# The up-projection's matmuls in six orders of 64-byte blocks, and operands at other distances from the weights

## The chip, the cores and the metric

The kernel runs on one core of a Trainium2 chip. The metric is the device time of one execution in microseconds (us). A core has a matrix engine (TensorE, "PE" in the profile, with "PEld" for its weight loads), a vector engine (VectorE, "DVE"), a scalar engine (ScalarE, "ACT"), GpSimd ("POOL") and a queue engine (SyncE, "SP") that issues the transfers. They work from an on-chip memory of 128 partitions; TensorE writes to the accumulation banks ("bank" and "sm" in the program), from which VectorE and ScalarE read.

## The reference

One layer of a decoder trunk on 256 tokens of width 2048, all float32. The sandwich of each sub-layer is norm, sub-layer, norm, residual:

```python
    h = rms_norm(x, ln_mix_pre[l])
    y = hybrid_mixer(h, positions, w_in[l], ...)          # four mixers, gates, w_branch, w_out
    x = x + rms_norm(y, ln_mix_post[l])
    h = rms_norm(x, ln_mem_q[l])
    y = memory_cross_attention(h, rms_norm(mem, ln_mem_kv[l]), mem_wq[l], mem_wkv[l], mem_wo[l])
    x = x + rms_norm(y, ln_mem_post[l])
    h = rms_norm(x, ln_ffn_pre[l])
    y = conv_ffn(h, ffn_w_up[l], ffn_conv_w[l], ffn_conv_b[l], ffn_w_down[l])
    x = x + rms_norm(y, ln_ffn_post[l])

def conv_ffn(h, w_up, w_conv, b_conv, w_down):
    u = causal_dwconv(h @ w_up, w_conv) + b_conv
    a, b = jnp.split(u, 2, axis=-1)
    return (jax.nn.gelu(a, approximate=True) * b) @ w_down
```

The up-projection `h @ w_up` is 2048 by 11264, in 88 chunks of 128 output channels.

## The kernel before

The kernel streams some 390 MB of weights once, in chunks of 2048 x 128 numbers (1 MB), numbered by `m` from the input projection to the down-projection. SyncE loads a chunk in two halves `h` of 512 KB into `raw`. ScalarE (L1274) rounds a half to the format `fp32r` ("high"), VectorE (L1977, in `low`) subtracts that from the original ("low"). Both parts go to one of four slots, `wsplit[(2 * m + h) % 4]`, each with 8 high blocks of 128 columns and 8 low ones. The activations are split likewise into 256 high and 256 low columns per block of 128 channels, side by side: `H` for the mixing stage, `X1` for W_out, the query projection and the up-projection, `X2` for the memory keys and the cross-attention's output projection (X2 also holds the memory that the values read).

There are two kinds of chunk. Where the weights are the stationary operand, a half is 8 wide matmuls (high weights times high and low activations, 512 columns, L543 in the mixing stage and L1008 behind it) and 8 narrow ones (low weights times high activations, 256 columns, L546 and L1017), added up in one accumulation bank. A chunk's halves run as high 0, low 0, low 1, high 1, so narrow and wide ones alternate in groups of sixteen. Where the output is wanted by tokens (retention values, gates, branches, memory values, down-projection), the activations are the stationary operand and the weights move: 512 columns each, L427 to L430, L1104 to L1106, L1221 to L1223.

The sequence on each engine is written out by hand, and semaphores tie them: `hi_done` and `lo_done` when a slot's part is ready, `half_used` when TensorE has read a half, `prod_out` when VectorE has taken a result out of its bank. The up-projection's chunks 0 and 1 are written apart (L1175 and L1178), 2 and 3 call `chunk`, and 84 more run in `loop(M_UP + 4, 21, X1)`, four chunks to a round. `chunk` calls `products`, that `high_products` and `low_products`.

Places are given in words of 4 bytes from `region_at`, a multiple of 1024 bytes. The slots start at 4096, 6144, 8192 and 10240, `H` at 12288, `X1` at 22288, `X2` at 35136. Blocks follow at 128 words in a slot, and at 512 words in an activation. Modulo 256 bytes all slots, H and X2 therefore lie at 0 and X1 at 64: the distance of the moving operand from the weights, modulo 256 bytes, is 64 with X1 and 0 with H and X2.

## Time and profile before

| | us |
|---|---|
| median of 3 runs (2188.47 to 2188.89) | 2188.55 |
| the profiled execution | 2189.49 |
| its span, first to last instruction | 2187.7 |
| TensorE busy in the span | 2161.2 |
| VectorE busy | 1439.2 |
| ScalarE busy | 1065.3 |
| wide matmuls of L1008, 2336 of them, busy | 563.9 |
| narrow matmuls of L1017, 2336 of them, busy | 296.4 |

The busy time of a group counts overlapping records once; the recorded duration of one matmul (392 ns for a wide one) reaches past the start of the next, since matmuls are pipelined. The distance from start to start tells what a matmul costs the engine: for sixteen in a row, the start of the group behind them minus their own.

### The profile page before, as it was taken

The page shows a single profiled execution, that of the slowest core. Times are in us where ns is not written, and L with a number is a line of the kernel's source. Part 1 is how long each engine was busy: PE and PEld are TensorE (multiplying, and loading weights), DVE is VectorE, ACT ScalarE, POOL GpSimd, SP SyncE. Part 2 cuts the span into 40 slices and gives each one's busy share as a digit, 9 for nine tenths or more (in the row PEclk, how much of TensorE's full clock was granted, in tenths as well). Part 3 has the DMA queues.
Part 4 walks back from the last instruction along what each step waited for, and adds up shares of the span by engine and source line. Part 5 has one row for each costly group of instructions (what it writes and reads, how often), then busy time and mean ns, then how long its engine had stood idle before and what let it go on. Part 6 is the DMA issues. An engine that isn't in the chain of part 4 may idle for free.

```text
span 2187.7 us, 33212 instructions
## 1 busy us (share of the span) xinstructions
PE 2161.2 (99%) x12606; PEld 1840.3 (84%) x12606; DVE 1439.2 (66%) x1651; ACT 1065.3 (49%) x1438; POOL 244.9 (11%) x220
## 2 busy tenths in 40 slices
PE   7999999999999999999999999989999999999998
PEld 6888888788888888888888888878888888888887
DVE  7986658676554546467765544578778777876444
ACT  6452245446444444445444444456656555644443
POOL 1132000000000101025110001312111111100000
PEclk9999999999999999999999999999999999999999
DMA  7543344445666665675556643636556555656664
GB/s 266 173 149 113 119 149 153 136 153 184 194 191 192 191 194 190 195 265 184 185 186 193 192 151 114 198 115 209 188 184 196 191 190 184 193 191 212 193 192 153
DMA packets 107071, 393.83 MB, mean 180 GB/s; under 512 B 11888, under 2 KB 12144, under 8 KB 106576
## 3 DMA queue, kind: packets, MB, share of 16 engines
q1 hardware_dynamic: 106672, 391.10, 55.5%
q8 instruction: 78, 1.28, 0.2%
q10 hardware_dynamic: 288, 1.18, 0.2%
q14 instruction: 33, 0.27, 0.0%
HBM read 390.14 MB, written 2.10 MB: 179 GB/s over the span
## 4 chain that ended last, share of the span: by engine, by line
PE 94%; DVE 3%; ACT 1%; DMA 1%; issue 1%; SPq 0%; DVEq 0%; ACTq 0%
PE bank L1008 24%; PE bank L1017 12%; PE bank L543 7%; PE sm L429 5%; PE sm L430 5%; PE sm L427 5%; PE bank L546 4%; PE bank L1221 3%; PE bank L1223 3%; PE bank L1222 3%; PE bank L427 2%; PE bank L429 2%; PE bank L430 2%; PE sm L595 2%; PE bank L1106 1%; PE bank L1105 1%
## 5 line engine op out<-in xcount | busy, mean ns | idle before, releaser
L1977 DVE TENSOR_TENSOR part<-part,part 128x1024 fp32r<-128x1024 f32 x724 | 933.5, 1292 | 527.6 <-ACT part L1274 516.7
L1274 ACT ACTIVATE part<-part 128x1024 fp32r<-128x1024 f32 x724 | 763.9, 1058 | 578.0 <-PE sm L430 177.6
L1008 PE MATMUL bank<-part,part 128*128 128x512 f32 x2336 | 563.9, 392 | 0.1
L1008 PEld LDWEIGHTS bank<-part,part 128*128 128x128 f32 x2336 | 427.9, 188 | 84.4 <-issue 0.5
L1017 PEld LDWEIGHTS bank<-part,part 128*128 128x128 f32 x2336 | 293.5, 188 | 12.4
L1017 PE MATMUL bank<-part,part 128*128 128x256 f32 x2336 | 296.4, 279 | 0.0
L543 PE MATMUL bank<-part,part 128*128 128x512 f32 x832 | 207.3, 396 | 0.9 <-DVE part L2032 0.8
L427 PE MATMUL sm<-part,part 128*128 128x512 f32 x512 | 199.2, 389 | 0.0
L429 PE MATMUL sm<-part,part 128*128 128x512 f32 x512 | 199.2, 389 | 0.0
L430 PE MATMUL sm<-part,part 128*128 128x512 f32 x512 | 199.2, 389 | 0.0
L543 PEld LDWEIGHTS bank<-part,part 128*128 128x128 f32 x832 | 151.5, 188 | 33.2 <-issue 2.1
L1596 ACT ACTIVATE part<-bank 128x256 f32<-128x256 f32 x152 | 58.1, 382 | 165.9 <-PE bank L1008 147.6
L1221 PE MATMUL bank<-part,part 128*128 128x512 f32 x352 | 137.2, 390 | 0.6 <-DVE part L2738 0.6
L1223 PE MATMUL bank<-part,part 128*128 128x512 f32 x352 | 137.0, 389 | 0.0
L1222 PE MATMUL bank<-part,part 128*128 128x512 f32 x352 | 136.9, 389 | 0.0
L546 PE MATMUL bank<-part,part 128*128 128x256 f32 x832 | 114.1, 286 | 2.5 <-DVE part L1977 2.4
L546 PEld LDWEIGHTS bank<-part,part 128*128 128x128 f32 x832 | 108.1, 191 | 9.8 <-issue 2.7
L427 PEld LDWEIGHTS sm<-part,part 128*128 128x128 f32 x512 | 96.1, 188 | 20.1
L429 PEld LDWEIGHTS sm<-part,part 128*128 128x128 f32 x512 | 96.1, 188 | 19.9
L430 PEld LDWEIGHTS sm<-part,part 128*128 128x128 f32 x512 | 96.1, 188 | 19.9
L2554 DVE TENSOR_TENSOR part<-bank,part 128x256 f32<-128x256 f32 x152 | 64.3, 423 | 71.9 <-ACT part L1596 71.6
L427 PE MATMUL bank<-part,part 128*128 128x512 f32 x224 | 90.3, 403 | 0.0
(382 smaller groups left out, 2204.4 us busy)
## 6 DMA issues: line engine op xcount, KB each, us to landing
part<-in_w_up SPq DMA_DIRECT2D x176, 512.0 KB, 4.5
part<-in_w_gate SPq DMA_DIRECT2D x128, 512.0 KB, 4.5
part<-in_w_dn SPq DMA_DIRECT2D x88, 512.0 KB, 4.5
part<-in_w_br SPq DMA_DIRECT2D x40, 512.0 KB, 4.5
part<-in_w_out SPq DMA_DIRECT2D x32, 512.0 KB, 4.7
part<-in_w_mk SPq DMA_DIRECT2D x32, 512.0 KB, 4.6
part<-in_w_mv SPq DMA_DIRECT2D x32, 512.0 KB, 4.2
part<-in_w_q SPq DMA_DIRECT2D x32, 512.0 KB, 4.3
```

What stands on the lines that cost most here:

```text
L427: pe.matmul(dst, xh, w[:, 0, j, :], start=first and h == 0 and j == 0, stop=False, skip_group_check=True)
L429: pe.matmul(dst, xh, w[:, 1, j, :], start=False, stop=False, skip_group_check=True)
L430: mm = pe.matmul(dst, xl, w[:, 0, j, :], start=False, stop=last and h == 1 and j == 1, skip_group_check=True)
L543: mm = pe.matmul(b, w[:, 0, k, :], H[:, 8 * h + k, :], start=h == 0 and k == 0, stop=h == 1 and k == 7, skip_group_check=True)
L546: mm = pe.matmul(b[:, T:2 * T], w[:, 1, k, :], H[:, 8 * h + k, 0:T], start=False, stop=False, skip_group_check=True)
L1008: mm = pe.matmul(dst, w[:, 0, k, :], x[:, k0 + k, :], start=start and k == 0, stop=stop and k == n - 1, skip_group_check=True)
L1017: mm = pe.matmul(dst[:, T:2 * T], w[:, 1, k, :], x[:, k0 + k, 0:T], start=False, stop=stop and k == n - 1, skip_group_check=True)
L1221: pe.matmul(bank[:, s, :], x, w[:, 0, j, :], start=k0 + j == 0, stop=False, skip_group_check=True)
L1222: pe.matmul(bank[:, s, :], x, w[:, 1, j, :], start=False, stop=False, skip_group_check=True)
L1223: mm = pe.matmul(bank[:, s, :], g[:, k + j, T + s * P:T + (s + 1) * P], w[:, 0, j, :], start=False, stop=k0 + j == FT - 1, skip_group_chec ...
L1274: act.activation(wsplit[(2 * m + h) % 4][:, 0, 0:n, :], raw[:, m % 2, h, 0:n, :], cp) .then_inc(sem("hi_done"), 1)
L1977: tt(w[:, 1, 0:n, :], raw[:, m % 2, h, 0:n, :], w[:, 0, 0:n, :].bitcast(f32), SUB).then_inc(sem("lo_done"), 1)
```

## The change

Three things are changed.

The orders: `chunk` and what it calls take a number `order`. `reordered` lays it over the moving operand and, in the same way, over the output, so that each column's sum lands where it did. Order 0 is the old one; 1 runs through all columns backwards; 2 swaps neighbouring blocks of 16 columns (64 bytes); 3 reverses each four blocks; 4 takes every fourth block, four times; 5 takes the even blocks, then the odd ones. The up-projection's loop runs 14 rounds of six chunks, one in each order, instead of 21 rounds of four.

The distances: a slot is now a place of 2112 words, and `parts` puts its contents at its start, or 48 words (192 bytes) behind it. At the start they lie in chunks in which the weights move (`by_tokens`, the compression chunks too) and in the second half of each chunk of the up-projection and of the first two of the down-projection. In all others they lie 192 bytes behind, and the distance of the moving operand is 64 bytes modulo 256. `X1` moves by 16 words, `X2` and others by 64 or 16, `raw` to 1024 bytes ahead of the region, and the region itself to a multiple of 256 bytes. So the first half of an up-projection chunk has the distance 64 and the second half 0; W_out and query chunks have 64 as before; the mixing chunks with H and the X2 chunks have 64 instead of 0.

Nothing is changed in what is loaded, split, waited for or written out.

```diff
+def by_tokens(m):
+    return m < NMIX and MIX[m][0] in ("rv", "gate", "br", "cmp") or M_MV <= m < M_WQ or m >= M_DOWN + 2
...
-        region_at = -(-nc.sbuf_base // 1024) * 1024
+        region_at = -(-nc.sbuf_base // 256) * 256 + 1024
...
-        raw = part(0, 2, 2, 8, P)
-        wsplit = [partr(8192, 2, 8, P), partr(10240, 2, 8, P), partr(4096, 2, 8, P), partr(6144, 2, 8, P)]
+        raw = part(-256, 2, 2, 8, P)
+        slots = [partr(a, 2112) for a in (8064, 10176, 3840, 5952)]
+
+        def parts(m, h):
+
+            s = slots[(2 * m + h) % 4]
+            aligned = by_tokens(m) or M_UP <= m < M_DOWN + 2 and h == 1
+            return (s[:, 0:2048] if aligned else s[:, 48:2096]).rearrange("p (l k c) -> p l k c", l=2, c=P)
...
-        X1 = partr(22288, KT, 2 * T)
+        X1 = partr(22272, KT, 2 * T)
...
-        X2 = partr(35136, 20, 2 * T)
+        X2 = partr(35072, 20, 2 * T)
...
+            def reordered(v, order):
+
+                if order == 1:
+                    return v[:, ::-1]
+                if order == 2:
+                    return v.rearrange("p (a b c) -> p a b c", b=2, c=16)[:, :, ::-1, :]
+                if order == 3:
+                    return v.rearrange("p (a b c) -> p a b c", b=4, c=16)[:, :, ::-1, :]
+                if order == 4:
+                    return v.rearrange("p (a b c) -> p b a c", b=4, c=16)
+                if order == 5:
+                    return v.rearrange("p (a b c) -> p b a c", b=2, c=16)
+                return v
...
-                w = wsplit[(2 * m + h) % 4]
+                w = parts(m, h)
                 for k in range(n):
-                    mm = pe.matmul(dst, w[:, 0, k, :], x[:, k0 + k, :], start=start and k == 0,
+                    mm = pe.matmul(reordered(dst, order), w[:, 0, k, :], reordered(x[:, k0 + k, :], order),
...
+                    mm = pe.matmul(reordered(dst[:, T:2 * T], order), w[:, 1, k, :],
+                                   reordered(x[:, k0 + k, 0:T], order), start=False,
...
-            loop(M_WO + 4, 3, X2)
+            loop(M_WO + 4, 3, X2, (0, 0, 0, 0))
...
-            loop(M_UP + 4, 21, X1)
+            loop(M_UP + 4, 14, X1, (0, 1, 2, 3, 4, 5))
```

TensorE's loop over the up-projection, a round's third and fourth chunk before (`part_68` is X1, `part_52` and `part_53` are the two slots of an odd chunk, `part_50` and `part_51` those of an even one):

```order
L1008 MATMUL bank<-part_68,part_50 128x512 x8
L1017 MATMUL bank<-part_68,part_50 128x256 x8
L1014 REGISTER_ALU
L1017 MATMUL bank<-part_68,part_51 128x256 x8
L1008 MATMUL bank<-part_68,part_51 128x512 x8
L1034 REGISTER_ALU
L1005 REGISTER_ALU
L1008 MATMUL bank<-part_68,part_52 128x512 x8
L1017 MATMUL bank<-part_68,part_52 128x256 x8
```

The same place in the changed kernel, a round's third chunk (order 2) and the start of its fourth (order 3):

```order
L1034 MATMUL bank<-part_68,part_50 128x16x2x16 x8
L1043 MATMUL bank<-part_68,part_50 128x8x2x16 x8
L1040 REGISTER_ALU
L1043 MATMUL bank<-part_68,part_51 128x8x2x16 x8
L1034 MATMUL bank<-part_68,part_51 128x16x2x16 x8
L1061 REGISTER_ALU
L1031 REGISTER_ALU
L1034 MATMUL bank<-part_68,part_52 128x8x4x16 x8
L1043 MATMUL bank<-part_68,part_52 128x4x4x16 x8
```

No instruction moves; only the operands' shapes become those of blocks (the reversed order reads like order 0 in such a row). The end of the round, changed kernel, orders 4 and 5:

```order
L1034 MATMUL bank<-part_68,part_50 128x4x8x16 x8
L1043 MATMUL bank<-part_68,part_50 128x4x4x16 x8
L1040 REGISTER_ALU
L1043 MATMUL bank<-part_68,part_51 128x4x4x16 x8
L1034 MATMUL bank<-part_68,part_51 128x4x8x16 x8
L1061 REGISTER_ALU
L1031 REGISTER_ALU
L1034 MATMUL bank<-part_68,part_52 128x2x16x16 x8
L1043 MATMUL bank<-part_68,part_52 128x2x8x16 x8
L1040 REGISTER_ALU
L1043 MATMUL bank<-part_68,part_53 128x2x8x16 x8
L1034 MATMUL bank<-part_68,part_53 128x2x16x16 x8
```

These two chunks follow four others in a round, where before the round ended after its fourth chunk.

## Rows read from the trace of the kernel before

**Rows 1.** the page: busy us (share of the span), granted clock by slice, chain by engine and line

```profile
PE 2161.2 (99%) x12606; PEld 1840.3 (84%) x12606; DVE 1439.2 (66%) x1651; ACT 1065.3 (49%) x1438; POOL 244.9 (11%) x220
PEclk9999999999999999999999999999999999999999
PE 94%; DVE 3%; ACT 1%; DMA 1%; issue 1%; SPq 0%; DVEq 0%; ACTq 0%
PE bank L1008 24%; PE bank L1017 12%; PE bank L543 7%; PE sm L429 5%; PE sm L430 5%; PE sm L427 5%; PE bank L546 4%; PE bank L1221 3%; PE bank L1223 3%; PE bank L1222 3%; PE bank L427 2%; PE bank L429 2%; PE bank L430 2%; PE sm L595 2%; PE bank L1106 1%; PE bank L1105 1%
```

**Rows 2.** busy us (count) of each engine in the up loop

```profile
core 0: us, PE busy (x) PEld busy (x) DVE busy (x) ACT busy (x) POOL busy (x), PEclk, DMA share, GB/s
1480.00:1938.00 458.00, 458.00 (x2658) 402.98 (x2657) 363.39 (x505) 274.15 (x418) 67.18 (x84) 1.00 0.60 192
```

**Rows 3.** waits in the same stretch: who for whom, us in total, times, longest

```profile
engine line waited for: us in total, times, longest us
...
DVE part L1977 <- ACT part L1274: 42.8, 72, 2.5
ACT part L1274 <- PE bank L1017: 37.0, 60, 0.9
```

**Rows 4.** TensorE in order of time, up loop (moving operand X1)

```profile
start us, us, engine line op out<-in xcount [idle before <-releaser]
1496.27 3.82 PE L1008 MATMUL bank<-part,part 128*128 128x512 f32 x16
1499.93 2.04 PE L1017 MATMUL bank<-part,part 128*128 128x256 f32 x16
1501.82 3.84 PE L1008 MATMUL bank<-part,part 128*128 128x512 f32 x16
1505.49 1.98 PE L1017 MATMUL bank<-part,part 128*128 128x256 f32 x16
1507.31 3.82 PE L1008 MATMUL bank<-part,part 128*128 128x512 f32 x16
1510.96 2.05 PE L1017 MATMUL bank<-part,part 128*128 128x256 f32 x16
1512.85 3.84 PE L1008 MATMUL bank<-part,part 128*128 128x512 f32 x16
1516.53 1.98 PE L1017 MATMUL bank<-part,part 128*128 128x256 f32 x16
1518.34 3.82 PE L1008 MATMUL bank<-part,part 128*128 128x512 f32 x16
1522.00 2.05 PE L1017 MATMUL bank<-part,part 128*128 128x256 f32 x16
```

**Rows 5.** the same, memory-key stage (moving operand X2)

```profile
1071.58 3.82 PE L1008 MATMUL bank<-part,part 128*128 128x512 f32 x16
1075.24 2.08 PE L1017 MATMUL bank<-part,part 128*128 128x256 f32 x16
1077.15 3.82 PE L1008 MATMUL bank<-part,part 128*128 128x512 f32 x16
1080.80 2.08 PE L1017 MATMUL bank<-part,part 128*128 128x256 f32 x16
1082.72 3.82 PE L1008 MATMUL bank<-part,part 128*128 128x512 f32 x16
```

**Rows 6.** the same, mixing stage (moving operand H)

```profile
484.89 3.82 PE L543 MATMUL bank<-part,part 128*128 128x512 f32 x16
488.55 2.08 PE L546 MATMUL bank<-part,part 128*128 128x256 f32 x16
490.46 3.82 PE L543 MATMUL bank<-part,part 128*128 128x512 f32 x16
494.11 2.08 PE L546 MATMUL bank<-part,part 128*128 128x256 f32 x16
```

**Rows 7.** the same, matmuls in which the weights are the moving operand

```profile
850.25 0.39 PE L427 MATMUL bank<-part,part 128*128 128x512 f32 x1
850.48 0.39 PE L429 MATMUL bank<-part,part 128*128 128x512 f32 x1
850.70 0.39 PE L430 MATMUL bank<-part,part 128*128 128x512 f32 x1
850.93 0.39 PE L427 MATMUL bank<-part,part 128*128 128x512 f32 x1
```

**Rows 8.** chain of 1338 to 1345 us, plain float32 matmuls: start, us, what

```profile
1340.62 3.47 PE sm L1127 x16
```

**Rows 9.** all weight loads of L1017: duration ns min/median/max, first and last start

```profile
L1017 PEld LDWEIGHTS bank<-part,part x2336: 187/188/192, 960.9 to 1937.4; 128*128 128x128 f32 x195
```

**Rows 10.** the wide matmuls of the mixing stage, whole span: busy us, mean ns | idle

```profile
L543 PE MATMUL bank<-part,part 128*128 128x512 f32 x832 | 207.3, 396 | 0.9 <-DVE part L2032 0.8
L555 PE MATMUL bank<-part,part 128*128 128x512 f32 x32 | 10.1, 466 | 8.8 <-ACT part L1274 8.3 <-DVE part L2090 0.5
```

**Rows 11.** chain of 1354 to 1361 us, groups of four after an interruption

```profile
1355.41 0.92 PE bank L1047 x4
1356.33 0.47 PE bank L1049 x4
1356.81 0.93 PE bank L1047 x4
1357.73 0.47 PE bank L1049 x4
1358.20 0.93 PE bank L1047 x4
```

More of the change, by code:

```diff
@@ L560, in first_low @@
                 for k in range(8 * h, 8 * h + 8):
-                    mm = pe.matmul(bank[:, n, T:2 * T], wsplit[2 * n + h][:, 1, k % 8, :], H[:, k, 0:T], start=False,
+                    mm = pe.matmul(bank[:, n, T:2 * T], parts(n, h)[:, 1, k % 8, :], H[:, k, 0:T], start=False,
                                    stop=h == 1 and k == 15, skip_group_check=True)
@@ L1034, in chunk @@
                 pe.wait_ge(prod_out, at(1, m - R_OFF - 1))
[L1035 removed]
+                products(m, at, x, 0, 8, x, 8, 8, bank[:, m % 2, :], split=split, order=order)
             def half(m, h, x, start=False, stop=False):
@@ L1067, in two_chunks, with loop @@
                 quarter(m + 1, 3, x).then_inc(half_used, 2)
-            def loop(base, count, x):
+            def loop(base, count, x, orders):
+                n = len(orders)
                 with pe.Fori(0, count) as i:
-                    for j in range(4):
-                        chunk(base + j, lambda k, v: i * (4 * k) + v, x)
+                    for j in range(n):
+                        chunk(base + j, lambda k, v: i * (n * k) + v, x, order=orders[j])
             def y_norm(value):
```

66 lines of the change are left out of this document (32 added, 34 removed).

## The prediction

> **What bounds the kernel now.** I began with the page's busy shares and chain [rows 1]: TensorE is busy for 2161.2 of 2187.7 us at full granted clock (2.4 GHz), and its matmuls are 94% of the chain. A matmul's recorded duration overlaps its successor's, so I work from starts. In the loop of the up-projection (1480 to 1938 us) TensorE is busy in all 458.00 us with 2658 matmuls, 32 to a chunk: 458/83.06 = 5.51 us a chunk [rows 2]. VectorE is busy 363 us there, ScalarE 274, the DMA engines 60%. Their own waits (VectorE L1977 for ScalarE 42.8 us, ScalarE L1274 for TensorE 37.0) show slack, and no wait of TensorE is in that list [rows 3]. So each nanosecond of a matmul's step, start to next start, is on the path, 16 times 512 columns and 16 times 256 per chunk.
>
> Three sets of steps matter. They differ in where the moving operand lies against the weights, counted in bytes modulo 256:
> - up loop, X1, +64 bytes. Starts 1505.49, 1507.31, 1510.96, 1512.85, 1516.53 [rows 4]: sixteen narrow steps 1.82, sixteen wide 3.65, then 1.89 and 3.68 (five chunks stand there, and they alternate so). Two chunks 11.04 us, **5.52 a chunk**.
> - memory-key stage, X2, 0 bytes: 3.66 and 1.91 each time, from 1071.58 to 1082.72 two chunks 11.14, **5.57 a chunk** [rows 5].
> - mixing stage, H, also 0 bytes: 1.91 and 3.65, together 5.56 [rows 6]. X2 is 256 bytes off H modulo 512, and behaves alike, so what counts repeats at 256 bytes or less.
>
> The same code, with VectorE and ScalarE as far from the bound in all three, costs 0.05 us more per chunk when the distance is 0. That is the only thing that the trace shows of the subject of the change.
>
> A step is longer than its columns. The weight-moving matmuls settle at 0.68 us for three, 226.7 ns [rows 7]: 544 cycles of 2.4 GHz for 512 columns, 32 too many. A plain-float32 256-column pass takes 3.47/16 = 217 ns, 521 cycles, 9 over twice 256 [rows 8]. So the extra belongs to moving at full rate beside a weight load (128 columns, 188 ns each [rows 9]). My reading, not shown: four blocks of 64 bytes are four banks, the two reads meet in one bank, and each gives way. If they meet by chance, a quarter of the 128 weight columns meet a moving one: 32 cycles, 13.3 ns, which is the excess of the 226.7 ns step. The 256-column step at distance 0, 1.91/16 = 119.4, has 13 ns over its 106.7 too.
>
> The Trainium skill speaks against this reading ("TensorE: Matmul & The Clock Gate", Part 2): the moving operand and the weights have independent read ports, and an isolated step is N/2.4 plus 2.5 ns. By that, as an estimate, a chunk would take 5.2 us, and distance and order would change nothing (rival 4). The two distances in [rows 4, 5] disagree.
>
> **The change, part by part.** TensorE's instructions, waits and their sequence stay; the loop's body is six chunks instead of four and it goes round 14 times instead of 21. The old wrap, every fourth chunk, leaves no mark in the five chunks of [rows 4], so wraps and register steps lie under queued matmuls: nothing. Region and slots move, transfers keep sizes: nothing, since the loads have slack. If that cover went, 14 wraps would cost some tenths of a us each.
>
> (a) Chunks outside the up-projection. 54 mixing chunks with H moving (832 + 32 wide matmuls / 16, [rows 10]) and 32 chunks with X2 go from distance 0 to +64. W_out and q chunks stay at +64, the weight-moving ones at 0. 86 x (5.52 - 5.57) = **-4.3 us**. The bounds: 0 if absolute place mattered and not distance; -86 x 0.10 = -8.6 if all went as the better pair of the up loop (1.82 + 3.65 = 5.47).
>
> (b) Up chunks in order 0: 4 before the loop and 14 in it. Their second half goes from +64 to 0: 18 x 0.05/2 = **+0.45 us**.
>
> (c) 70 chunks in orders 1 to 5 (reversed; neighbouring blocks swapped; four blocks reversed; every fourth block; every second block), half of each at either distance. No row has such an operand. The nearest are the straight ones, and they bound it thus: best seen pair 5.47, so -0.05 x 70 = -3.5; worst seen, the groups of four right after an interruption [rows 11], 0.93 and 0.47 or 0.48 for four: 4 x 1.41 = 5.64, +0.12 x 70 = +8.4. I take the value of distance 0, 5.57, because by counting meetings (a quarter of the weight columns) it is what any order gives that is not tuned to its neighbour, while +64 is a relation that holds only for two ascending streams: 70 x 0.05 = **+3.5 us**.
>
> Sum: -4.3 + 0.45 + 3.5 = -0.35 us. The profiled execution (2189.49 us, span 2187.7 and 1.8 around it) would become 2189.1; the median of the runs, 2188.55, becomes **2188.2**.
>
> **Rivals.**
> 1. Faster: some orders keep the streams apart. Order 5 reads only even banks in its first half, order 4 stays in one bank for 4 or 8 blocks while the weights walk through all. If these 70 chunks run as the best pair (-3.5 instead of +3.5) the total is -4.3 + 0.45 - 3.5 = -7.35: 2181.2. If the excess of the wide steps halved too (6.7 ns x 16 = 0.11 us a chunk more, 7.5 in all), -15: 2173.7. For: distance alone already moves 0.05 to 0.10 us. Against: the meetings are only shifted, both streams must still visit every bank.
> 2. Slower, weights late: in orders 4 and 5 the moving read sits on the weights' bank for long, the load of the next weights ends late, and the narrow matmuls wait, since their step (114 to 119 ns) is far shorter than a load's 188 ns [rows 9], which now overlaps its neighbour. At worst a narrow step becomes 188: (188 - 115.6) x 16 = 1.16 us, x 28 chunks = +32 us: 2220. A third of it, if the load only loses the blocks that it shares: +11: 2199. It decides, against a bound of 0.2%, once the mean narrow step of the five orders is 4 ns over the 119 that I take (4.7 us over 1120 narrow steps).
> 3. Slower, the pattern itself: a descending or a jumping operand is read or written at half rate, as plain float32 moves (217 ns for 256 columns [rows 8]). For the reversed order alone: a wide step 434, a narrow 217, a chunk 10.4: +4.9 x 14 = +68 us: 2256. If every block jump cost one cycle more (0.42 ns), 32 and 16 jumps a matmul: 16 x 48 x 0.42 = 0.32 us x 56 chunks = +18: 2206. The rows have no such operand, for or against.
> The Trainium skill has the rule behind rival 3 ("PSUM — Partial Sum Buffer", Specifications (TRN2)): cachelines of 8 bytes, and any non-contiguous pattern slows matmuls significantly. No run here shows it; runs of 64 bytes fill whole lines, so I weigh it low except for the reversed order.
> 4. The change does nothing: what I ascribe to distance belongs to the stage, (a) is 0 and (b), (c) too: 2188.5.
>
> **How the numbers follow.** Forecast (net -4 to +3 us) 0.42; rival 1 0.22; rival 2 0.18; rival 3 0.14; rival 4 0.04. Rival 1 ends beyond the bound of 0.2% (4.4 us, about what a measurement of this kernel can tell from no change) in nearly all its cases, and so does the edge of the forecast at times: faster 0.24. Same: forecast and rival 4, with the mild end of 2: 0.47. Slower: the rest of 2 and 3: 0.29. The range, 2180 to 2208, holds the forecast, rivals 1 (its -7.35), 4, the third of 2 and the block-jump case of 3 and leaves out the full lateness and the half rate. The likeliest case's own range is 2184.5 to 2192.
>
> **What would show it.** In the changed profile: mixing chunks outside interruptions, starts 5.52 apart instead of 5.56 (a); order-0 chunks between 5.52 and 5.57 (b); the chunk lengths in the up loop repeating with period six, all within 5.47 to 5.64 (c), and the stretch of the loop near 84 x 5.55 = 466 us. Rival 1 is shown by orders below 5.47, rival 2 by narrow steps over 125 ns in the last two of each six with wide ones unchanged, rival 3 by one chunk in six far above. I'd be wrong if (a) doesn't appear, or if one order costs or gives over 0.3 us a chunk.

## The result, and the profile after

| | before | after |
|---|---|---|
| median of 4 runs each, us | 2188.51 | 2197.95 (2197.53 to 2198.81) |
| ratio, 95% interval | | 1.0044 (1.0032 to 1.0056) |
| profiled execution, us (span) | 2189.49 (2187.7) | 2197.94 (2196.2) |
| TensorE busy, us | 2161.2 | 2169.5 |
| loop of the up-projection (84 chunks), us | 463.41 | 475.86 |

The change costs 9.4 us, 0.44%. The forecast was 2188.2 us, 0.3 us less than before. The time lies inside the stated range (2180 to 2208) but outside the likeliest case's own (2184.5 to 2192), and beyond the bound of 0.2% on the slower side, to which the prediction gave a chance of 0.29.

The page of the changed kernel, TensorE's share, its granted clock, and the chain by engine and line, answering [rows 1]:

```profile
PE 2169.5 (99%) x12606; PEld 1840.8 (84%) x12606; DVE 1439.2 (66%) x1651; ACT 1064.1 (48%) x1438; POOL 245.9 (11%) x220
PEclk9999999999999999999999999999999999999999
PE 92%; DVE 4%; ACT 1%; issue 1%; DMA 1%; SPq 0%; DVEq 0%; ACTq 0%
```

TensorE is busy 8.3 us longer with the same 12606 matmuls, VectorE not a microsecond. So the time went into the matmuls themselves. In the up loop (columns as in [rows 2]) there are still no gaps, and answering [rows 3] the same two waits stand in the list, none of them TensorE's:

```profile
core 0: us, PE busy (x) PEld busy (x) DVE busy (x) ACT busy (x) POOL busy (x), PEclk, DMA share, GB/s
1477.00:1937.00 460.00, 460.00 (x2599) 399.12 (x2598) 354.69 (x491) 266.35 (x409) 65.08 (x82) 1.00 0.58 187
```

```profile
DVE part L2005 <- ACT part L1302: 48.7, 80, 2.4
ACT part L1302 <- PE bank L1043: 42.8, 58, 1.0
```

2599 matmuls are 81.2 chunks: 460/81.2 = 5.66 us a chunk where [rows 2] gave 5.51. TensorE in order of time in that loop, answering [rows 4]; L1034 are the wide matmuls, L1043 the narrow ones. The narrow row that starts at 1507.59 belongs to a chunk of order 0, the ones below it to orders 1, 2, 3, 4, 5 and 0 again:

```profile
1507.59 2.06 PE L1043 MATMUL bank<-part,part 128*128 128x256 f32 x16
1509.48 3.87 PE L1034 MATMUL bank<-part,part 128*128 128x512 f32 x16
1513.19 2.07 PE L1043 MATMUL bank<-part,part 128*128 128x256 f32 x16
1515.10 3.90 PE L1034 MATMUL bank<-part,part 128*128 128x512 f32 x16
1518.83 2.07 PE L1043 MATMUL bank<-part,part 128*128 128x256 f32 x16
1520.74 3.94 PE L1034 MATMUL bank<-part,part 128*128 128x512 f32 x16
1524.52 2.07 PE L1043 MATMUL bank<-part,part 128*128 128x256 f32 x16
1526.42 3.93 PE L1034 MATMUL bank<-part,part 128*128 128x512 f32 x16
1530.19 2.05 PE L1043 MATMUL bank<-part,part 128*128 128x256 f32 x16
1532.08 3.98 PE L1034 MATMUL bank<-part,part 128*128 128x512 f32 x16
1535.90 2.09 PE L1043 MATMUL bank<-part,part 128*128 128x256 f32 x16
1537.82 3.92 PE L1034 MATMUL bank<-part,part 128*128 128x512 f32 x16
1541.59 2.06 PE L1043 MATMUL bank<-part,part 128*128 128x256 f32 x16
```

Six chunks take 1541.59 - 1507.59 = 34.00 us, 5.667 each. Sixteen narrow steps are 1.89 to 1.92 us throughout, 118 to 120 ns. Sixteen wide ones, which were 3.65 to 3.68, are 3.71, 3.73, 3.78, 3.77, 3.82, 3.77: the longest is around order 5. From the starts of all 84 chunks, the mean length by order is:

| order | 0 | 1 | 2 | 3 | 4 | 5 |
|---|---|---|---|---|---|---|
| us a chunk | 5.576 | 5.638 | 5.662 | 5.674 | 5.685 | 5.755 |

The memory-key stage, answering [rows 5], went the other way, from 5.57 to two chunks in 1078.02 - 1066.98 = 11.04, 5.52 each; the mixing stage, answering [rows 6], now has a pair of 488.11 - 486.30 = 1.81 and 491.77 - 488.11 = 3.66, where before it had 1.91 and 3.65:

```profile
1066.98 2.05 PE L1043 MATMUL bank<-part,part 128*128 128x256 f32 x16
1068.87 3.84 PE L1034 MATMUL bank<-part,part 128*128 128x512 f32 x16
1072.55 1.98 PE L1043 MATMUL bank<-part,part 128*128 128x256 f32 x16
1074.36 3.82 PE L1034 MATMUL bank<-part,part 128*128 128x512 f32 x16
1078.02 2.04 PE L1043 MATMUL bank<-part,part 128*128 128x256 f32 x16
...
486.30 1.98 PE L558 MATMUL bank<-part,part 128*128 128x256 f32 x16
488.11 3.82 PE L555 MATMUL bank<-part,part 128*128 128x512 f32 x16
491.77 2.05 PE L558 MATMUL bank<-part,part 128*128 128x256 f32 x16
```

Matching the matmuls of both executions one by one, the changed kernel is 4.29 us ahead at matmul 8826, shortly before the up-projection's loop, and 8.4 behind at the end. Of these 12.7 us the loop lost 475.86 - 463.41 = 12.45.

### The profile page after: what moved, and what is told of

The parts are those of the page before. It is cut to its first block, busy times and chain, and to the rows that moved or that the text cites. A ratio compares the mean times of both kernels' runs of the same rounds, so it can differ in the third digit from the quotient of the medians.

```text
span 2196.2 us, 33198 instructions
## 1 busy us (share of the span) xinstructions
PE 2169.5 (99%) x12606; PEld 1840.8 (84%) x12606; DVE 1439.2 (66%) x1651; ACT 1064.1 (48%) x1438; POOL 245.9 (11%) x220
## 4 chain that ended last, share of the span: by engine, by line
PE 92%; DVE 4%; ACT 1%; issue 1%; DMA 1%; SPq 0%; DVEq 0%; ACTq 0%
PE bank L1034 24%; PE bank L1043 12%; PE bank L555 6%; PE sm L439 5%; PE sm L442 5%; PE sm L441 5%; PE bank L1249 3%; PE bank L1250 3%; PE bank L1251 3%; PE bank L558 3%; PE bank L439 2%; PE bank L441 2%; PE bank L442 2%; PE sm L607 2%; DVE part L2005 1%; PE bank L1132 1%
## 5 line engine op out<-in xcount | busy, mean ns | idle before, releaser
L1034 PE MATMUL bank<-part,part 128*128 128x512 f32 x2336 | 572.0, 396 | 0.1
L1034 PEld LDWEIGHTS bank<-part,part 128*128 128x128 f32 x2336 | 428.5, 188 | 91.0 <-issue 0.5
L1043 PEld LDWEIGHTS bank<-part,part 128*128 128x128 f32 x2336 | 296.1, 188 | 13.2
L1043 PE MATMUL bank<-part,part 128*128 128x256 f32 x2336 | 299.3, 280 | 0.0
```

The lines of the kernel that those rows point to most:

```text
L1034: mm = pe.matmul(reordered(dst, order), w[:, 0, k, :], reordered(x[:, k0 + k, :], order), start=start and k == 0, stop=stop and k == n - 1 ...
L1043: mm = pe.matmul(reordered(dst[:, T:2 * T], order), w[:, 1, k, :], reordered(x[:, k0 + k, 0:T], order), start=False, stop=stop and k == n ...
```

## The experiments

All kernels start from the changed one. "Chunk" is us per chunk in the up loop, from starts (mean or median, which differ by 0.02 at most); "wide" and "narrow" are steps in ns, start to next start, averaged over sixteen in a row where nothing else is said (512 and 256 columns: 213.3 and 106.7 at 2.4 GHz; the granted clock was full in all). All these matmuls have `fp32r` operands. Each kernel was timed beside the kernel before, whose medians were 2188.2 to 2188.8. A kernel of which no ratio is given was timed once.

### Which part of the change costs: plain_split, plain_far, each_order

```diff
 plain_split:
-            loop(M_UP + 4, 14, X1, (0, 1, 2, 3, 4, 5))
+            loop(M_UP + 4, 14, X1, (0, 0, 0, 0, 0, 0))
 plain_far: that, and
-            aligned = by_tokens(m) or M_UP <= m < M_DOWN + 2 and h == 1
+            aligned = by_tokens(m)
 each_order:
-            loop(M_UP + 4, 14, X1, (0, 1, 2, 3, 4, 5))
+            for g in range(6):
+                loop(M_UP + 4 + 14 * g, 7, X1, (g, g))
```

> The changed kernel with all six chunks of a round in order 0; places and distances as in the change (first half of an up-projection chunk at 64 bytes, second half at 0). Theory A (the orders cost, the distances do what the straight rows say): the gain outside the up-projection, 4.3 us, stays; the up-projection's chunk takes 5.567 us or a little under; total 2184.2 + 88 x 0.05 at most = 2184 to 2188.5. Theory B (mixing two distances in one chunk costs by itself, as order 0 in the change, 5.576 us a chunk, hints): 5.58 a chunk, 2189.

> Order 0 everywhere, and both halves of every up-projection chunk at distance 64: only the places of the change outside the up-projection are left. Theory A (only the distance modulo 256 bytes counts, not the absolute place): chunks alternate 5.476 and 5.559 us as before, 2188.5 - 4.3 = 2184.2, 0.998 of before. Theory B (absolute places count too): the loop is not 463.4 us, and the total anywhere in 2184 to 2192.

> The change with the same 84 chunks, but each order in 14 chunks in a row (six loops of 7 rounds of two) and not one after another. Theory A (the cost belongs to the order's own pattern against the weights): the same chunk lengths as in the change within 0.03 us: 5.58, 5.64, 5.66, 5.67, 5.69, 5.76 us; total 2198. Theory B (the cost comes from the step from one order to the next, groups of 16 that never settle): chunks near 5.57, total near 2189.

Measured: plain_split 2187.69 us (ratio 0.9993, 0.9984 to 1.0002), chunk 5.540. plain_far 2185.66 (0.9987, 0.9978 to 0.9996), chunk 5.517. each_order 2200.66, loop 475.78, chunks by order 5.540, 5.640, 5.687, 5.680, 5.680, 5.760.

The first 14 chunks of each_order (order 0) run as in plain_split. Three rows from its fourteen chunks of order 5:

```profile
1887.66 3.99 PE L1034 MATMUL bank<-part,part 128*128 128x512 f32 x16
1891.49 2.09 PE L1043 MATMUL bank<-part,part 128*128 128x256 f32 x16
1893.42 3.99 PE L1034 MATMUL bank<-part,part 128*128 128x512 f32 x16
```

1893.42 - 1887.66 = 5.76, wide (1891.49 - 1887.66)/16 = 239.4. So each order has its own price, which is not one of the transition between orders: 84 chunks took 475.78 us in blocks and 475.86 mixed. The distance of 64 bytes is a small gain (0.05 us a chunk). Without the orders the new places are worth 4.25 us by the trace of plain_far at the start of the loop, which is what (a) of the prediction says. By the medians of the whole time they are worth 3.1 us, less than the 4.3 expected.

### Reading or writing: read_only, write_only

```diff
 read_only (each_order, and):
-pe.matmul(reordered(dst, order), w[:, 0, k, :], reordered(x[:, k0 + k, :], order),
+pe.matmul(dst, w[:, 0, k, :], reordered(x[:, k0 + k, :], order),
 write_only (each_order, and):
+pe.matmul(reordered(dst, order), w[:, 0, k, :], x[:, k0 + k, :],
```

(the narrow matmuls likewise)

> The six orders in 14 chunks each, as in each_order, but laid over the moving operand only; the output is written straight, so each sum lands in the wrong column. Theory A (the cost is in the read, where it meets the weights' read): the chunk lengths of each_order, 5.54, 5.64, 5.69, 5.68, 5.68, 5.76 us. Theory B (the cost is in the jumping write into the accumulation bank): 5.54 in all.

> The counterpart: the orders are laid over the output only, the moving operand is read straight; the sums land in wrong columns. Theory A: 5.54 us in all six groups, the loop 465.4 us. Theory B: the chunk lengths of each_order, and the loop 475.8 us. If both share it, the excess over 5.54 here and in read_only add up to that of each_order.

Measured: read_only 2199.51 us, every order as in each_order. write_only 2187.86, chunk 5.540 in all six; this is the same place in it:

```profile
1885.68 3.84 PE L1034 MATMUL bank<-part,part 128*128 128x512 f32 x16
1889.36 2.03 PE L1043 MATMUL bank<-part,part 128*128 128x256 f32 x16
1891.22 3.84 PE L1034 MATMUL bank<-part,part 128*128 128x512 f32 x16
```

The whole cost is in reading the moving operand. Writing PSUM in blocks of 64 bytes in any of these orders costs nothing. The Trainium skill ("PSUM — Partial Sum Buffer", Specifications (TRN2)) warns that any non-contiguous pattern slows matmuls significantly; for runs of 64 bytes, and for a reversed write of single columns (order 1), this run shows no slowing.

### Do the two reads meet in a bank: bank_map, dist_a, dist_b, pairs_a

My theory was that 64-byte blocks are dealt to four banks and that weight load and moving read hinder each other where they meet. bank_map reads chosen blocks only, the one-column weights too out of `X1`:

```diff
-                    mm = pe.matmul(reordered(dst, order), w[:, 0, k, :], reordered(x[:, k0 + k, :], order),
+                    w, v = picked(m, h, 0, k, x, k0 + k, 2 * T, order)
+                    mm = pe.matmul(dst, w, v,
```

> Leaves out the up-projection's right products: in 84 chunks the operands are read from chosen 64-byte blocks of each 256 bytes (called bank 0 to 3), output straight. 14 chunks each: (1) weights by steps of 256 bytes, all in bank 0, moving operand in bank 2 only; (2) both in bank 0; (3) weights in bank 0, moving straight; (4) weights straight, moving in bank 0 only; (5) weights straight, moving in banks 0 and 1; (6) weights in bank 0, moving in bank 1. Theory A (four banks of 64 bytes, reads of weights and moving operand meet in a bank and give way): (1) and (6) lose the excess, wide steps under 219 ns and narrow under 112; (2) meets at each of 128 weight columns: wide 260 to 280, narrow 150 to 200; (3), (4), (5) near 227 to 240. Theory B (no banks, a fixed price of a weight load beside a full-rate stream): 227 and 120 in all six, or one price for strided weights in 1, 2, 3 and 6 alike.

| group | weights from | moving from | wide, ns | narrow, ns | chunk |
|---|---|---|---|---|---|
| 1 | block 0 of each 256 bytes, one column in each | block 2 | 243 | 204 to 217 | 7.360 |
| 2 | as 1 | block 0 | 262 to 279 | 228 to 243 | 8.093 |
| 3 | as 1 | straight | 234 to 247 | 210 to 224 | 7.313 |
| 4 | straight | block 0 | 242 | 123 | 5.847 |
| 5 | straight | blocks 0 and 1 | 236.5 | 120 | 5.707 |
| 6 | as 1 | block 1 | 243 | 204 to 217 | 7.360 |

The time was 2305.53 us. In groups 1 and 6 the 243 ns are the common single step; the first wide step behind narrow ones takes 338, so the mean of sixteen is 249.5.

Both from the same block (2) costs 0.73 us a chunk over different blocks (1), so meeting is real. Kept fully apart (1, 6) the wide step was still 243 ns, not 213. That alone doesn't show that meeting isn't what a straight read pays for, since neither operand was read straight there: weights taken one column from every 256 bytes make narrow steps of 204 to 217 ns with any moving operand, and a moving operand in jumping blocks costs 240 ns by itself (pairs_a below). load_cols is the better test.

The distances were then tried with straight reads, one distance for each stage (a constant offset in the function parts):

> Order 0 everywhere; the weights lie at another distance in each stage (moving operand minus weights, modulo 256 bytes): mixing 96, W_out 0, memory keys 128, query 192, cross-attention output 64, up-projection 32. Theory A (two ascending streams meet as their distance says): 0 gives 5.57 us a chunk, 64 alternates 5.476 and 5.559 wherever it stands, the others between 5.44 and 5.64, and no two stages at one distance differ. Theory B (it is the stage that sets the length): each stage keeps its old length.

> Order 0, other distances: mixing 48, W_out 80, memory keys 16, query 224, cross-attention output 160, up-projection 96 bytes. Theory A: neighbours of 64 (48, 80) lie between 64 (5.52 us a chunk) and 32 or 96 (5.60 and 5.65); 16 between 0 (5.57) and 32; 96 in the up-projection is what it was in the mixing stage of dist_a (233.3 and 120). Theory C: the distance moves the narrow step only, since that alone is near the load's own time; wide ones stay 226.7 to 233.4.

| bytes modulo 256 | 0 | 16 | 32 | 48 | 64 | 80 | 96 | 128 | 160 | 192 | 224 |
|---|---|---|---|---|---|---|---|---|---|---|---|
| wide, ns | 228.4 | 228.6 | 233.3 | 231.7 | 229.4 | 230.6 | 233.2 | 232.6 | 233.9 | 233.0 | 233.1 |
| narrow, ns | 119.6 | 119.7 | 116.7 | 116.8 | 113.3 to 117.8 | 117.8 | 120.1 | 118.7 | 118.6 | 113.7 | 118.6 |

(dist_a 2198.67 us, dist_b 2203.49.) No distance is free; 64 bytes is the best sum, by little. It is the distance that counts and not the stage: W_out, which had 64 bytes before, took the 228.4 and 119.5 ns of the memory keys once it stood at 0. At distance 0 two single wide steps of three are 226.7 ns, and in pairs_a nearly all are 240.0: 2 and 4 times 6.67 ns over 213.3, where 6.67 ns are sixteen columns at 2.4 GHz, one block. But at 32 bytes the single steps lie at 230 to 235, so this is a hint and no rule. pairs_a reads blocks i and i+16 in turn, to test whether two reads in step lock into each other's way at some distances and not at others:

```diff
+                if order == 6:
+                    return v.rearrange("p (a b c) -> p b a c", a=2, c=16)
```

> A new order in all plain chunks of W_out, memory keys, query, cross-attention output and up-projection: block i and block i + 16 (i + 8 in narrow matmuls) one after the other, so that the moving operand goes round the four banks at half its pace, which is the pace of the weights' read. Distances as in dist_a: 0, 128, 192, 64 and 32 bytes in these stages. Theory A: locked in step, the streams never meet at 128 (memory keys): wide 214 to 219 ns, narrow 108 to 113, chunk 5.15 to 5.35 us; at 0 they always meet and it is the worst, 5.7 or more. Theory B (any jumping order costs by its jumps): 5.68 to 5.76 at every distance.

Measured: 2222.35 us, and 240.0 and 120.0 ns at each of the five distances (0, 128, 192, 64, 32). Here the distance decides nothing. The lock-step theory fell: it needed a distance at which this order is cheap.

### What the excess depends on: load_cols, mv_width

```diff
 load_cols:
-                    mm = pe.matmul(reordered(dst, order), w[:, 0, k, :], ...
+                    mm = pe.matmul(reordered(dst[0:c], order), w[:, 0, k, 0:c], ...
 mv_width:
+                    mm = pe.matmul(dst[:, 0:wide], w[:, 0, k, :], x[:, k0 + k, 0:wide],
```

> Leaves out part of the up-projection's output channels: 14 chunks each with 96, 64 and 32 weight columns in order 0, then 64 and 32 columns in the order of pairs, then 64 in order 5; distance 0. Theory A (the excess is made by the weights' read beside the moving one): it shrinks with the weight columns: wide 223, 220, 217 ns in order 0, pairs 227 and 220. Theory C (new: the moving stream alone loses a cycle of 0.42 ns at each change of a 64-byte block, another at each jump; this fits 226.7 = 213.3 + 32 x 0.42, and 240.0 with 32 jumps): the wide steps stay at 226.7, and at 240.0 in pairs, whatever the load's length.

> Leaves out part of the tokens: wide matmuls of 448, 384, 320, 256 columns with narrow ones of 256, then 512 with narrow ones of 192 and 128; order 0, distance 0. Theory A (an excess per load, as long as the load is over before the step): wide 200.0, 173.3, 146.7, 120 ns, that is columns / 2.4 GHz plus 13.3; the narrow ones of 192 and 128 bound by the load at 112 to 125. Theory C (17 cycles per 16 columns): 198.3, 170.0, 141.7, 113.3.

Measured, load_cols (2196.04 us): 96, 64 and 32 weight columns with straight reads 5.540, 5.493 and 5.527 us a chunk (wide 230, 229.7, 231); 64 and 32 columns in pairs 5.760 (240.0 and 120.0, to the tenth); 64 columns in order 5 5.747. Loads of a quarter of the columns (108 ns each in the trace and not 188) leave the excess as it is, so it is no count of weight columns met. My count (a quarter of 128 columns, 32 cycles) matched 13.3 ns by coincidence. mv_width (2147.83 us): 512, 448, 384 and 320 columns step in 227 to 230, 203, 173.3 and 146.7 ns, each 13 to 17 over columns/2.4. So from 320 to 512 columns the excess is about the same for each matmul and doesn't grow with the columns of a straight read. That also speaks against the other theory, a cycle lost at each 64-byte block: it fits the 240.0 of the pairs, but wanted 141.7 ns at 320 columns. Narrow matmuls of 192 and 128 columns still stepped in 110 and 108 ns, where 80 and 53 would do by their columns. So something else than the moving columns sets these, the runs don't tell what, and the excess is best read from the wide steps. (In the groups of 320 and 256 columns some chunks waited for VectorE, so for 320 the commonest single step is given.)

### Runs of which length: run_len

```diff
+                    if order:
+                        v = v.rearrange("p (a b c) -> p b a c", a=2, c=order)
+                    mm = pe.matmul(dst, w[:, 0, k, :], v,
```

> Reads the moving operand's two halves alternately in runs of 4, 8, 32, 64, 128 and 1 columns (the output straight, so sums land in wrong columns), distance 0; runs of 16 are the order of pairs, 240.0 ns wide. Theory A (meetings): runs of 32 and more behave like straight ones or like another distance, 227 to 234, and short runs do not matter as such: 233 to 243. Theory C (a cycle at each jump): 280, 253, 233.3, 230.0, 227.9 and for single columns far more, 440.

| run, columns | 4 | 8 | 32 | 64 | 128 | 1 |
|---|---|---|---|---|---|---|
| chunk, us | 6.027 | 5.867 | 5.683 | 5.567 | 5.567 | **5.240** |
| wide / narrow, ns | 250 / 126.6 | 243.3 / 123.3 | 236 / 119 | 228.4 / 119.5 | 228.4 / 119.5 | **216.0 / 111.5** |

The time was 2198.27 us. Reading one column from each half in turn came out faster than the straight read, which I had not expected, and which fits neither of the expectation's theories. TensorE in that group:

```profile
1898.59 3.62 PE L1037 MATMUL bank<-part,part 128*128 128x512 f32 x16
1902.04 1.95 PE L1049 MATMUL bank<-part,part 128*128 128x256 f32 x16
1903.83 3.62 PE L1037 MATMUL bank<-part,part 128*128 128x512 f32 x16
```

1903.83 - 1898.59 = 5.24. The Trainium skill's isolated step ("TensorE: Matmul & The Clock Gate", Part 2), N/2.4 plus 2.5 ns, would be 215.8 and 109.2 as an estimate: alternation is the first order in which a trace of this case comes near it (216.0, 111.5), and the wide straight reads stay 11 to 18 ns above it. That these depend on the distance from the weights disagrees with the independent read ports that the Trainium skill states there.

### Which property makes it free: alt_kinds, alt_near

Both read the moving operand in six orders, 14 chunks each, write straight, and have the weights at distance 0.

```diff
 alt_kinds, group 2 (every 2nd column) and 6 (neighbouring blocks in turn):
+                    return v.rearrange("p (c a) -> p a c", a=2)
+                    return v.rearrange("p (b a c) -> p b c a", a=2, c=16)
 alt_near, group 3 and 4 (2 and 4 columns apart in turn):
+                    return v.rearrange("p (b a c) -> p b c a", a=2, c=2)
+                    return v.rearrange("p (b a c) -> p b c a", a=2, c=4)
```

> Weights at distance 0, the output written straight, the moving operand of the up-projection's loop read in six orders, 14 chunks each. What is left out: the putting back of the columns, so the sums of these chunks stand in other columns. Orders: (1) two columns from each half in turn, (2) the even columns, then the odd ones, (3) every 4th column, four times, (4) every 16th column, 16 times, so that each column is in another 64-byte block than the one before, (5) one column from each of the four quarters in turn, (6) one column from each of two neighbouring 64-byte blocks in turn. run_len gave 5.240 us a chunk for one column of each half in turn, 6.027 for four, 5.867 for eight. Theory (what costs is a fetch of a 64-byte block beside a fetch of weights: a read that takes less than a block's worth at each jump is never served by block, so (2) to (6) are free of it, about 5.24; (1) is 5.24 or, if two columns are still a run, 6.1 or more). Rival (the reads of single columns are free only where both blocks stay the same for 16 steps): (5) and (6) 5.24 as alternation, (2), (3) near 5.54, (4) over 6.

> As alt_kinds (weights at distance 0, straight output, the sums of the loop's chunks left in other columns than the reference's where the order is not straight), in six other orders of reading, 14 chunks each: (1) straight, but written down as pairs of columns, (2) each pair read backwards (1, 0, 3, 2, ...), (3) two columns 2 apart in turn (0, 2, 1, 3, 4, 6, ...), (4) 4 apart (0, 4, 1, 5, ...), (5) 8 apart, (6) one column from each of four neighbouring 64-byte blocks in turn. So far one column of two places in turn took 5.240 us a chunk with the places 16, 128 or 256 columns apart, straight 5.54, four places 128 apart 6.83. Theory A (it is the alternation between two places, however near, that avoids the excess): (2) to (5) 5.24, (1) 5.54 since it is the straight read; (6) 6.8. Theory B (it is the form of the pattern, an innermost dimension of two elements): (1) too at 5.24. Theory C (the two places must lie in different 64-byte blocks): (2) to (5) at 5.54 or more. For (6), 5.24 would say that what made the four places slow was how far apart they were.

The times were 2459.75 us (alt_kinds) and 2193.32 (alt_near).

| order of reading | kernel, group | wide / narrow, ns | chunk |
|---|---|---|---|
| straight, written as pairs | alt_near 1 | 228.4 / 119.5 | 5.567 |
| each pair backwards | alt_near 2 | the same | 5.567 |
| two columns in turn, 2 apart | alt_near 3 | the same | 5.567 |
| 4 apart | alt_near 4 | 215.9 / 111.5 | 5.240 |
| 8 apart | alt_near 5 | 215.9 / 111.5 | 5.240 |
| 16 apart (neighbouring blocks) | alt_kinds 6 | 215.9 / 111.5 | 5.240 |
| two columns from each half in turn | alt_kinds 1 | 328 / 165 | 7.893 |
| one from each of four quarters | alt_kinds 5 | 283 / 143 | 6.827 |
| one from each of four neighbouring blocks | alt_near 6 | 269 / 135.6 | 6.471 |
| every 2nd / 4th / 16th column | alt_kinds 2, 3, 4 | 451 / 461 / 433 | 10.847 / 11.113 / 10.453 |

TensorE in alt_near, group 3, then group 4:

```profile
1692.65 3.82 PE L1036 MATMUL bank<-part,part 128*128 128x512 f32 x16
1696.30 2.08 PE L1045 MATMUL bank<-part,part 128*128 128x256 f32 x16
1698.22 3.82 PE L1036 MATMUL bank<-part,part 128*128 128x512 f32 x16
...
1724.85 3.62 PE L1036 MATMUL bank<-part,part 128*128 128x512 f32 x16
1728.31 1.95 PE L1045 MATMUL bank<-part,part 128*128 128x256 f32 x16
1730.09 3.19 PE L1036 MATMUL bank<-part,part 128*128 128x512 f32 x14
```

Of alt_near's three theories, B (the form of the pattern) falls by groups 2 and 3, which are written in the same form as 4 and gain nothing. A (any alternation) falls by the same two. C (different 64-byte blocks) falls by groups 4 and 5, which stay within a block and are free. What the runs leave is a bound on distance: two places in turn are free of the excess at 4 columns (16 bytes) apart and at each larger distance tried (8, 16, 128, 256), and like a straight read at 2; 3 was not tried. Four places in turn cost 53 to 67 ns a wide step, runs of two columns 112, and a regular stride of 2, 4 or 16 columns about as much as a second read of the whole operand (451 against 213). alt_kinds' theory, that every read of single columns would be free, is refuted.

### The whole kernel with alternating reads: alt_plain, alt_every, alt_dist, alt_zero

```diff
 alt_plain (from plain_far):
+        def alternate(v):
+            return v.rearrange("p (h a c) -> p h c a", a=2, c=P)
-pe.matmul(reordered(dst, order), w[:, 0, k, :], reordered(x[:, k0 + k, :], order),
+pe.matmul(dst, w[:, 0, k, :], alternate(x[:, k0 + k, :]),
-                tt(dst, bank[:, b:b + 1, 0:T], cross[:, b:b + 1, :], ADD)
+                tt(dst.rearrange("p o (a c) -> p (o c) a", a=2), pairs(bank[:, b:b + 1, 0:T]),
+                   pairs(cross[:, b:b + 1, :]), ADD)
 alt_every (also):
+        def turns(v):
+            return v.rearrange("p (a c) -> p c a", a=2)
-pe.matmul(dst, xh, w[:, 0, j, :],
+pe.matmul(dst, xh, turns(w[:, 0, j, :]),
-ts(rv[:, 0, quad * 512:quad * 512 + 512], bank[:, 0, :], rcol[:, 0:1], None, MUL)
+ts(turns(rv[:, 0, quad * 512:quad * 512 + 512]), pairs(bank[:, 0, :]), rcol[:, 0:1], None, MUL)
```

(pairs is the same view without the exchange, "p (c a) -> p c a". The other matmuls of the chunks that the expectations name, and the operations that take their sums out of PSUM, are edited likewise.)

> Order 0 in the loop and both halves 64 bytes from the weights, as in the kernel plain_far (2185.66 us). Every matmul whose moving operand is activations (the mixing, W_out, memory-key, W_Q, W_O and up-projection chunks) reads that operand one column from the first 128 tokens and one from the next 128, in turn, and writes straight; the vector engine's add at the end of a chunk puts the columns back in order as it writes them. Nothing is left out. Theory (a read that alternates single columns runs without the excess at every place, 216.0 and 111.5 ns as in the last group of run_len against 229 and 115 ns): 5.24 us a chunk against 5.517, so 0.28 us less in some 200 chunks, about 56 us, 2130 us. Rival (the excess was absent only because the weights of run_len stood at distance 0, or because that group followed another): 2180 to 2186 us. Second rival (the vector engine's strided write makes the chunks wait): between 2150 and 2200 us, with chunks over 5.4 us.

> As alt_plain, and the token matmuls too (retention values, gates, branches, memory values, down-projection; there the weights are the moving operand, 512 columns) read their moving operand one column from the first 256 and one from the next 256, in turn; the operations that take the sums out of PSUM put the columns back. Nothing is left out. Theory (the excess goes from every fp32 matmul that alternates columns): 226.7 to 216.0 ns in 3648 token matmuls, 39 us less than alt_plain, about 2090 us. Rival (in those the vector or scalar engine, or the memory, sets the pace): within 10 us of alt_plain.

> As alt_every, with the weights of the chunks at other distances (in bytes, modulo 256): mixing 160, W_out 0, memory keys 128, W_Q 64, W_O 32, up-projection 224. Theory (without block fetches the distance decides nothing): 216.0 and 111.5 ns at each of them, the time within 2 us of alt_every. Rival (the distance decides as before): a chunk between 5.24 and 5.6 us, other in every stage, and the time 10 to 40 us above alt_every.

> As alt_every (2101.57 us), with all weights at distance 0 as in the kernel before, so that alternation is the only difference from it that can matter. Theory (alternation alone brings the gain, the distance nothing beside it): 2101 to 2103 us, 5.240 us a chunk. Rival (the distance of 64 bytes gives a part of it): about 2105 us or more, by the 4.3 us that it gave to straight reads.

| kernel | median, us | ratio (95%) | chunk, us | VectorE busy, us |
|---|---|---|---|---|
| alt_plain | 2139.22 | 0.9777 (0.9760 to 0.9793) | 5.240 | 1468.3 |
| alt_every | 2101.57 | 0.9602 (0.9586 to 0.9618) | 5.240 | 1474.0 |
| alt_dist (one run) | 2101.60 | | 5.240 | 1474.4 |
| alt_zero | **2101.31** | **0.9602 (0.9586 to 0.9618)** | 5.240 | 1474.0 |

In alt_zero, whose weights all stand at distance 0 as before the change, the up loop reads:

```profile
1502.94 3.62 PE L1046 MATMUL bank<-part,part 128*128 128x512 f32 x16
1506.40 1.95 PE L1055 MATMUL bank<-part,part 128*128 128x256 f32 x16
1508.18 3.62 PE L1046 MATMUL bank<-part,part 128*128 128x512 f32 x16
```

The median steps of sixteen in a row are 216.0 and 111.5 ns in every stage of all four kernels, at all seven distances that they contain (alt_dist's expectation counts from the other operand; in the counting of the table above they are 96, 0, 128, 192, 224 and 32, with alt_plain's 64). So with alternating reads the distance is worth nothing, and alt_zero, the simplest, is as fast as any: 4.0% or 87 us faster than the kernel before.

alt_plain came 9 us short of the 2130 that I expected. The up loop gave all that was expected: 463.40 to 440.35 us, 84 x 0.274. The rest went into waits. By the pages TensorE is idle for 2183.9 - 2157.4 = 26.5 us of the span in plain_far and for 2136.9 - 2102.0 = 34.9 in alt_plain, 8.4 us more. In the mixing stage, where, matmul by matmul against plain_far, 54 chunks gave 8.9 us and not 54 x 0.274 = 14.8, TensorE's busy time in the first 492 us fell from 479.98 to 474.35 with more matmuls done: 5.6 us more idle, nearly all of it for VectorE. TensorE's waits for VectorE there, plain_far, then alt_plain (us in total, times, longest):

```profile
PE bank L558 <- DVE part L2005: 2.1, 2, 1.6
PE bank L555 <- DVE part L2060: 1.0, 2, 0.9
PE sm L832 <- DVE part L2408: 0.5, 2, 0.3
...
PE bank L562 <- DVE part L2009: 3.4, 3, 1.8
PE bank L559 <- DVE part L2065: 3.1, 4, 1.3
PE sm L836 <- DVE part L2413: 2.0, 3, 0.9
```

That is the expectation's second rival, in small. Of the remaining 3 us, 1.8 are lost in the memory-key stage, 1.09 of them in one gap behind VectorE's add at the end of a chunk (TensorE in alt_plain, last bracket: idle us before, releaser):

```profile
1102.56 1.89 PE L1038 MATMUL bank<-part,part 128*128 128x512 f32 x8
1105.55 1.99 PE L1038 MATMUL bank<-part,part 128*128 128x512 f32 x8 [1.09 <-DVE part L2588]
```

That add is the price of alternating, since it writes in pairs 128 columns apart. The line's instructions in alt_every, ns min/median/max:

```profile
L2597 DVE TENSOR_TENSOR part<-bank,part x152: 600/626/640, 938.3 to 1864.2; 128x256 f32<-128x256 f32 x152
```

and in plain_far:

```profile
L2582 DVE TENSOR_TENSOR part<-bank,part x152: 409/425/426, 968.0 to 1935.8; 128x256 f32<-128x256 f32 x152
```

152 x 0.2 = 30 us more on VectorE in these, and 11 us more in the mixing stage's 54 adds (418 to 614 ns each). That is 41 us by recorded durations, which overlap; VectorE's busy time rose by 30 us, and TensorE's idle time, as said, by 8.4. alt_every gave 2139.22 - 2101.57 = 37.7 us more, for 39 expected.

## Why the prediction was wrong, point by point

- **What bounds the kernel** held: each nanosecond of a matmul's step showed in the time, in both directions (475.86 us of loop, and 440.35).
- **(a), -4.3 us for 86 chunks that go to distance 64**: the traces give -4.29 by the start of the up-projection. Right, and the time confirms its sign: plain_far 2185.66 us.
- **(b), +0.45 us for order 0**: I took 5.545 us a chunk; by itself it is 5.540 (each_order), next to the other orders 5.576. It was about 0.6 us too low.
- **(c), +3.5 us for 70 chunks in orders 1 to 5: this is the step that failed.** I took 5.57 us, the value of distance 0, with a bound of 5.64. Measured were 5.638, 5.662, 5.674, 5.685 and 5.755, on average 5.683: 70 x (5.683 - 5.517) = +11.6 us. Four of the five lie above my upper bound. With -4.3 and 18 x 0.059 = 1.1 for order 0 that makes +8.4; the profiled executions differ by 2197.94 - 2189.49 = 8.45.
- **Why (c) failed.** The term was mis-sized by 8 us. The choice of 5.57 rested on counting meetings of weight columns and moving blocks. The count gave the right 13.3 ns for straight reads, but load_cols shows that the number of weight columns makes no difference to it, and mv_width that it hardly changes from 320 to 512 columns. From an accounting that fits by coincidence I inferred that no order could be worse than chance. The bound 5.64 came from straight reads too: no row of before had another order, and a bound taken from rows of another kind was no bound.
- **Rival 3 (the pattern itself)** was nearest in mechanism: reading blocks out of order costs something per matmul, and its 2206 us lies 8 us off, the forecast 10. But it isn't a price for each jump: order 1, which runs backwards and never jumps, costs nearly as much as orders 2 to 4. What it named for the reversed order, half rate, didn't come: 5.638 us a chunk and not 10.4. Half rate exists, but for regular strides of single columns (alt_kinds).
- **Rival 2 (late weights)** named a time of 2199 us, 1 us from the measured one, but by luck; it is refuted. Narrow steps are 118 to 120 ns, about the 119 that I took, the loads take 188 as in [rows 9], and in load_cols loads of 64 and 32 columns leave the pairs at 240.0 ns:

```profile
L1043 PEld LDWEIGHTS bank<-part,part x2336: 187/188/193, 958.5 to 1945.5; 128*128 128x128 f32 x195
```

- **Rival 1 (some orders keep the streams apart)**: none of the five does. But that an order can be better than straight was right in a form that I hadn't thought of, by single columns and not by blocks. **Rival 4 (nothing)** is refuted by (a).
- **The Trainium skill** ("TensorE: Matmul & The Clock Gate", Part 2), which I set against my reading, is right about the step that is possible (5.2 us a chunk by its formula, 5.240 measured) and wrong about this kernel's straight reads (5.52 to 5.65). I used the disagreement only as a rival of no effect, when it also said that 0.3 us a chunk were to be had.

**What stays open**: why a read has the excess at all. Settled by runs are that it belongs to the read of the moving operand and not to the write, to the transition between orders or to late weights; that it hardly changes with the length of the load or, from 320 to 512 columns, with the width of the read, and depends on the distance from the weights for straight reads; and that two places in turn, at the distances tried from 16 bytes up, have none of it. A mechanism that gives all of these, with the high price of four places and of strides, I don't have. Whether the straight read has the excess without a weight load beside it was not tried, nor whether operands in another format have it.

## What to carry to other kernels

When TensorE is gapless, compare the step between starts of matmuls with columns over the clock; if steps of wide `fp32r` matmuls stand 10 ns or more above it, read the moving operand as two places in turn, one column each, at least 16 bytes apart, write PSUM straight, and put the columns back in the operation that takes the sums out of PSUM. That operation gets longer, so look for new waits where chunks are short of slack. Here all of it was worth 4%, while placing operands at a chosen distance was worth 0.13% and nothing beside it. Don't bound an operation by rows of another form: an order of access that the trace doesn't show can be cheaper or twice as dear, and one kernel with six forms in a loop prices them all in one run.

## What the runs showed of the hardware

- An `fp32r` matmul of 512 columns with weights loaded beside it steps in 228 to 234 ns for straight reads, in up to 240 for reads in permuted blocks of 64 bytes, and in 216.0 ns when single columns of two places alternate (256 columns: 113 to 121 and 111.5), at full granted clock.
- Two places in turn: 2 columns apart 228.4 ns, 4, 8, 16, 128 or 256 apart 216. Runs of 2, 4, 8, 16 and 32 columns from two places: 328, 250, 243, 240, 236. Four places: 269 to 283. Every 2nd, 4th or 16th column: 451, 461, 433.
- Reading the moving operand backwards costs 4 ns a wide step and 2.5 a narrow one, writing PSUM backwards or in permuted 64-byte blocks nothing.
- Weights taken one column from every 256 bytes make a narrow step of 204 to 217 ns instead of 115 to 120 (210 to 224 beside a straight read), and their loads are recorded with 290 to 340 ns instead of 188.
- An add from PSUM of 256 columns on VectorE took 425 ns with a straight write and 626 with a write that alternates between two places 512 bytes apart.
